# Hybrid mLSTM/attention/MoE trunk: the router reads the residual row without its norm, between the blocks of the output projection, and the slot lists are built by one-hot matmuls

## What is computed

```python
x = post_norm(x, concat([ya, yb, yc]) @ w_out[l], g_a, ln_g[l, 0], ln_b[l, 0])   # LayerNorm(ALPHA*x + gate*y)
h = x * (1.0 + sc_f) + sh_f
x = post_norm(x, moe_ffn(h, w_router_grp[l], w_router_exp[l], ...), g_f, ln_g[l, 1], ln_b[l, 1])

def moe_ffn(h, w_rg, w_re, w_g, w_u, w_d):
    pg = softmax(h @ w_rg); grp = argmax(pg); g_w = max(pg)          # 1 of 4 groups
    le = (h @ w_re).reshape(T, 4, 8)[own group]
    top_l, top_i = top_k(le, 2); top_w = softmax(top_l) * g_w        # 2 of its 8 experts
    ...                       # each expert: (silu(xb @ w_g[e]) * (xb @ w_u[e])) @ w_d[e], on its own tokens
    y = segment_sum(out[pos] * w_s)
```

## Time and profile before

| | |
|---|---|
| median of 3 runs | 1881.56 us (1878.47 to 1889.72) |
| the profiled execution | 1880.61 us |
| its span | 1878.7 us, 22715 instructions |
| PE matmul busy | 1457.2 us (78%) |
| PE weight load busy | 1014.3 us (54%) |
| DVE / ACT / POOL busy | 605.1 / 338.9 / 411.3 us |
| chain that ended last, by engine | PE 61%, DMA 19%, DVE 10%, issue 4%, POOL 3% |

### The profile page before, as it was taken

How to read it: one execution, slowest core, us unless ns; L and a number is a source line. 1 busy time by engine, 2 the same in 40 slices (tenths; PEclk the granted TensorE clock), 3 DMA queues, 4 the chain that set the end, 5 groups by cost and what they waited for, 6 DMA issues and landing times.

```text
span 1878.7 us, 22715 instructions
## 1 busy us (share of the span) xinstructions
PE 1457.2 (78%) x8398; PEld 1014.3 (54%) x8398; DVE 605.1 (32%) x1375; ACT 338.9 (18%) x854; POOL 411.3 (22%) x552
## 2 busy tenths in 40 slices
PE   5999999687973798897049999978798548998730
PEld 2888888465862333332048888855587514333210
DVE  0301232764353112111542123247725412111144
ACT  0211112463010111111012111225511001111001
POOL 1000041522172111111130000525215231112113
PEclk9999999799965899998579999989898569999865
DMA  9112436125053699996412133431123529999832
GB/s 354 49 72 76 165 118 238 48 76 192 11 221 149 234 407 412 396 394 274 165 45 76 54 121 136 171 121 43 35 90 140 229 102 377 418 399 410 343 122 100
DMA packets 76252, 356.19 MB, mean 190 GB/s; under 512 B 21776, under 2 KB 25008, under 8 KB 41200
## 3 DMA queue, kind: packets, MB, share of 16 engines
q1 hardware_dynamic: 41040, 291.63, 39.3%
q0 software_dynamic: 22528, 48.74, 7.6%
q10 hardware_dynamic: 12576, 14.37, 2.4%
HBM read 344.28 MB, written 33.16 MB: 201 GB/s over the span
## 4 chain that ended last, share of the span: by engine, by line
PE 61%; DMA 19%; DVE 10%; issue 4%; POOL 3%; ACT 1%; SPq 1%; DVEq 0%; POOLq 0%; ACTq 0%
PE bank L894 22%; PE bank L1188 10%; PE bank L1105 7%; DMA att<-h_rows,cur 7%; DMA ring<-in_w_exp 4%; PE bank L1207 3%; PE bank L697 2%; PE bank L1172 2%; DMA z<-expert_rows 2%; DMA ring<-in_w_ada 2%; PE bank L1052 1%; DMA att<-bias_full 1%; PE bank L712 1%; PE bank L1126 1%; DMA z<-in_w_exp 1%
## 5 line engine op out<-in xcount | busy, mean ns | idle before, releaser
L894 PE MATMUL bank<-ring,hT 128*128 128x256 f32 (+1 forms) x1920 | 411.3, 373 | 3.6 <-DVE hT L1585 3.6
L894 PEld LDWEIGHTS bank<-ring,hT 128*128 128x128 f32 x1920 | 350.5, 190 | 48.2 <-issue 5.2
L1188 PE MATMUL bank<-ring,att 128*64 128x512 f32 (+1 forms) x512 | 166.0, 635 | 19.8 <-DMA ring<-in_w_exp 19.8
L1105 PE MATMUL bank<-ring,hT 128*128 128x256 f32 x640 | 138.6, 379 | 2.4 <-issue 2.4
L1105 PEld LDWEIGHTS bank<-ring,hT 128*128 128x128 f32 x640 | 121.4, 190 | 19.0 <-issue 2.6
L1188 PE MATMUL bank<-z,att 128*64 128x512 f32 x512 | 121.4, 629 | 11.5 <-DMA z<-in_w_exp 11.4
L1188 PEld LDWEIGHTS bank<-ring,att 128*64 128x64 f32 (+1 forms) x512 | 61.6, 168 | 109.8 <-issue 109.8
L2077 DVE TENSOR_TENSOR att<-att,bank 128x256 f32<-128x256 f32 x38 | 16.0, 421 | 304.9 <-ACT att L1512 304.9
L1757 DVE COPY z<-bank 128x512 f32<-128x512 f32 (+3 forms) x36 | 21.0, 583 | 260.0 <-PE bank L894 260.0
L2345 POOL COPY cur<-att 128x1 int32<-128x1 int32 (+1 forms) x38 | 6.9, 181 | 392.9 <-ACT att L1519 293.8
L1172 PE MATMUL bank<-const,att 128*128 128x128 f32 x320 | 52.7, 319 | 43.4 <-DMA att<-h_rows,cur 41.6
(11 more groups left out here) (319 smaller groups left out, 2112.9 us busy)
## 6 DMA issues: line engine op xcount, KB each, us to landing
ring<-in_w_exp SPq DMA_DIRECT2D x96, 1024.0 KB, 15.8
z<-in_w_exp SPq DMA_DIRECT2D x96, 1024.0 KB, 13.6
ring<-in_w_ada SPq DMA_DIRECT2D x48, 1024.0 KB, 5.0
ring<-in_w_in SPq DMA_DIRECT2D x24, 1024.0 KB, 7.0
z<-expert_rows ACTq DMA_DIRECT2D x20, 512.0 KB, 4.3
ring<-in_w_out SPq DMA_DIRECT2D x8, 1024.0 KB, 10.2
z<-mod_rows POOLq DMA_DIRECT2D x12, 512.0 KB, 8.6
h_rows<-z POOLq DMA_DIRECT2D x10, 512.0 KB, 2.9
```

Of the source, the lines that this page charges most:

```text
L894: last = eng.matmul(bk[:, i * UN:i * UN + nw], hTv[:, k, t * P:(t + 1) * P], w[:, k, 0:nw], start=(k == 0), stop=(k == KD - 1))
L1105: last = eng.matmul(bk[:, i * UN:(i + 1) * UN], hTv[:, k, t * P:(t + 1) * P], w[2 * half + i][:, k, :], start=(k == 0), stop=(k == KD - 1))
L1188: last = eng.matmul(bank[2 + j][c * m_:(c + 1) * m_, :], e["xT"][:, j, k * P + c * m_:k * P + (c + 1) * m_], wv[c][:, 0:2, k, :], start=(k ...
```

## The change

**The router reads x without its norm.** With u = ALPHA*x + gate*y, the row h is linear in u for a given mean and rstd, so h @ w = rstd * (u @ W') - mean*rstd * colsum(W') + b'w, with W' = w times ln_g*(1+sc_f) and b' = ln_b*(1+sc_f) + sh_f. `router_weights` makes the two scaled copies of the router weights for the two kinds of rows (`lr["wx"]`) on DVE in the attention loop behind unit 4. `router_sums` takes their column sums on PE (8 matmuls of 144 columns) at i = 16. ln_g and ln_b in column form come from a transpose at the start of the program. RT now transposes x itself as soon as u is there, and RL multiplies by wx.

**Order.** PE does RT and RL of tile t-1 between the blocks of the projection of tile t. The choice of experts is made in two parts: tiles 0 to 3 (`choose(0)`) on DVE between the two residuals of tile 4, tile 4 (`choose(1)`) behind its logits. The rank matmuls are in two parts too, the first 10 between RT and RL of tile 4, with wider moving operands (6 of 64 to 128 columns, 4 of one), and 3 after the second choice.

**Rows for the experts.** POOL folds ln_g and ln_b into the scale and shift rows once (6 products and sums of 1024, event `rows`); then h comes from the centred row in two operations. `ln_gain` and `ln_shift` of tiles 3 and 4 are moved behind the slots and behind the first two gathers, the loads of the next norm rows too. The final routing weights (`weights_of_two`) are made last.

**Slot lists.** Slot numbers are compared with multiples of 128 (which pass) and with 0..127 (which place); 10 matmuls of a 128x128 one-hot by a 128x31 one-hot times (token number + 1) sum up to the transposed lists in PSUM. The DRAM lists, their first fill and their 10 scatters are gone.

**Loads.** SP issues expert weights 2 when u of tile 4 and `rows` are there, and weights 3 when the last RL is full. Two masks now come to z by two loads at the start, and ACT's first copy waits for them in place of the fill of the DRAM lists.

```diff
-                eng.wait_ge(*ev.at("full", jobs.number(("RL", l, NT - 1))))
-                eng.wait_ge(*ev.at("st_h2", l, NT - 2))
-                eng.wait_ge(*ev.at("st_h2", l, NT - 1))
+                eng.wait_ge(*ev.at("u", l, NT - 1))
+                eng.wait_ge(*ev.at("rows", l))
...
+                    if n == 3:
+                        eng.wait_ge(*ev.at("full", jobs.number(("RL", l, NT - 1))))
...
+                def rows_turned(t):
...
+                        eng.wait_ge(*ev.at("u", l, t))
                         for k in range(4):
-                            last = eng.transpose(bk[:, k * P:(k + 1) * P],
-                                                 m["hs"][:, t % 2, (4 * j + k) * P:(4 * j + k + 1) * P], ident)
+                            last = eng.transpose(bk[:, k * P:(k + 1) * P], x[:, t, (4 * j + k) * P:(4 * j + k + 1) * P], ident)
...
+                for t in range(NT):
+                    for half in range(2):
+                        jobs.open("Y", l, t, half)
+                        eng.wait_ge(*jobs.room())
+                        project(t, half, 0)
+                        if half == 0 and t > 0:
+                            rows_turned(t - 1)
+                        project(t, half, 1)
+                        if half == 0 and t > 0:
+                            logits(t - 1)
+                rows_turned(NT - 1)
+                ranks(0)
+                logits(NT - 1)
+                ranks(1)
...
+                for k in range(2):
+                    eng.wait_ge(*ev.at("hot", l, k))
+                    for t in range(NT):
+                        n = k * NT + t
+                        last = eng.matmul(bk[:, 0:NLIST], hot["slot"][:, n, :], hot["pass"][:, n, :], start=(n == 0),
+                                          stop=(n == 2 * NT - 1))
...
+            def router_weights(l):
...
+                for part, col in enumerate((gcol, bcol)):
+                    for g in range(2):
+                        last = eng.tensor_tensor(lr["wx"][:, :, 2 * part + g, :], wr[:, :, :], bc(col[:, g, :], 2, 36), ALU.mult)
...
                 for t in range(NT):
+                    if t > 0:
+                        turned_half(t - 1)
+                        logit_fix(t - 1)
+                    residual(t, 0)
+                    if t > 0:
+                        logit_rows(t - 1)
+                    if 0 < t < NT - 1:
+                        expert_rows(t - 1)
+                        ln_gain(1, t - 1)
+                    if t == NT - 1:
+                        choose(0)
+                    residual(t, 1)
+                    ln_stats(1, t)
+                turned_half(NT - 1)
+                logit_fix(NT - 1)
+                expert_rows(NT - 2)
+                logit_rows(NT - 1)
+                choose(1)
+                expert_rows(NT - 1)
...
-                eng.tensor_copy(posi[:, :], s5[:, 8:10, :].rearrange("p a b -> p (a b)")).then_inc(*dve.event("slots", l))
+                eng.tensor_tensor(hot["ge"], bc(at, 2, 32), bc(K["iopass"], 1, 2 * NT), ALU.is_ge).then_inc(*dve.step())
...
+                    eng.tensor_tensor(hot["slot"][:, ns, :], bc(within[:, ns], 2, P), bc(K["iop"], 1, NT),
+                                      ALU.is_equal).then_inc(*dve.event("hot", l, k))
...
+                for g in range(2):
+                    eng.tensor_tensor(m["free"][:, g, :], lr["scsh"][:, 0, g, :], m["ln"][:, 1, :], ALU.mult).then_inc(*pool.step())
+                    eng.wait_ge(*pool.last())
+                    eng.tensor_tensor(lr["scsh"][:, 1, g, :], lr["scsh"][:, 1, g, :], m["free"][:, g, :], ALU.add)
+                    last = eng.tensor_tensor(lr["scsh"][:, 0, g, :], lr["scsh"][:, 0, g, :], m["ln"][:, 0, :], ALU.mult)
+                last.then_inc(*pool.event("rows", l))
...
                 for t in range(NT):
+                    if 0 <= t - 1 < NT - 2:
+                        store_rows(t - 1)
+                    ln_rstd(1, t)
+                    if 0 <= t - 1 < NT - 2:
+                        ln_shift(1, t - 1)
+                store_rows(NT - 2)
...
-                for q in range(2 * NT):
-                    eng.indirect_dma_start(list_dram[l], bass.IndirectOffsetOnAxis(ap=posi[:, q:q + 1], axis=0),
-                                           ids[:, q:q + 1], None).then_inc(*pool.event("list_in", l, q, by=16, sem="list_in"))
-                eng.wait_ge(*ev.at("list_in", l, 2 * NT - 1))
-                ld(listi, list_dram[l].rearrange("(b p) o -> b (p o)", p=P), "list_back", l)
```

458 lines of the change are left out of this document (262 added, 196 removed).

## The result

| | before | changed |
|---|---|---|
| median | 1883.22 us (4 runs, 1878.47 to 1889.72) | 1823.88 us (4 runs, 1821.26 to 1824.33) |
| ratio | | 0.9682, 95% interval 0.9658 to 0.9706 |
| span of the profiled execution | 1878.7 us | 1819.4 us |

The account below looks back on a forecast made before the run. PE, busy 78% of the span, was taken as the bound. Projection to first pass: 119.2 us against 157.4; less 3.5 for attention, 34.7 gained per layer, 69.1 in all with the start: 1812 us, range 1796 to 1835.

Parts of the forecast that it names:

- Projection, 83 us at clock 1.00: Sign of being right: the projection with four RT and four RL inside takes 83 us at full clock.
- The first tile, 1.5 us: Early in the projection, PE stalls ahead of RT(1) for u(1), behind POOL's first rstd: about 1.5 us, 0 to 6.
- waits of 1 to 2 us are harmless to the clock: In the projection, planned PE waits of 1 to 2 us lie below what the trace shows to be harmless.
- Clock halved throughout (the other side): Rival: transposes between projection matmuls halve PE's clock; throughout, 69.3 us more per layer, 1951 us; chance 0.05.
- No interleaving: Rival: in the projection RL takes 3.6 us, POOL's six operations 3.21 each; +11 us per layer, 1834 us; chance 0.12.
- The split: choose(0), at most 5.7 us on DVE, hides behind 6.9 us of projection; its failure (1823 us) is within the 0.66.
- Ranks at E + 12.1: Behind the projection's end (E), the ranks are ready after 12.1 us, where before it was 55.6.
- Slots at E + 20.5: After the ranks, the same 8.4 us of short PE/DVE exchanges put the slots 20.5 us behind the projection's end (E).
- Lists, 8.5 us: From slots to slot lists, DVE comparisons and ten one-hot matmuls at half clock take 8.5 us, before 18.4.
- First gather: From lists to first pass, 5.7 us before plus 1.5 for busy DMA; first pass 36.2 us behind the projection's end.
- the DMA rival: Rival: weight loads, stores of h and gather collide ahead of the first pass; +9 us per layer, 1830 us; chance 0.13.
- Gain outside: In the attention, router_weights (+1.5) and router_sums (+2.0) cost 3.5 us per layer, bounds 1.5 and 6.

Follow-up runs that it names:

- e3: Changed kernel with POOL adding the shift of the expert rows of tiles 3 and 4 on only 64 of 1024 columns: 1820.5 us.
- e4: Changed kernel with the load of the fourth weight buffer waiting for the first gather's landing in place of the last logits: 1824.2 us.

## Why the prediction was right, and where it was off

- **The sign and the mechanism.** Right. Both parts undone one at a time give it back: the place of the router 19 us per layer with the split choice (5.4 at the ranks) in it, the lists 15. They add up to 34, beside the 33.6 and 33.2 gained between the start of the projection and the first pass; but each was undone with the other in place, so this sum could as well have missed. That the router reads the row without its norm was not undone alone; it is what allows the place.
- **Projection, 83 us at clock 1.00.** RT 0.87 to 1.04 and RL 1.71 to 1.87 us stood against 1.04 and 2.0 in the sum; 79.9 us without any stall, 81.5 predicted. The measured 83.9 and 85.0 come from the term of the first tile.
- **The first tile, 1.5 us.** The wait was 2.07 and 2.98 us, within its bounds of 0 to 6, but the term's own pieces don't give its 1.5: rstd at 28 and 5.8 us of DVE work make u(1) 33.8, ahead of PE's 34.2. In layer 0 rstd came at 28.5 and u(1) at 35.9; most of what the pieces lacked is the hold of 1.4 us on the second residual, by POOL's addition for tile 0. And the sentence that waits of 1 to 2 us are harmless to the clock failed. It rested on the earlier trace rows, where the clock fell 4.5 us (I read 5) after dense work ended; that showed when it falls in a long pause, not that a short one is safe. Each fall cost 1.7 us, and each wait 0.2 beyond its length. Term 1.5, measured 3.9 and 4.9.
- **Clock halved throughout (the other side).** Refuted: 1.00 over the whole projection where no wait stands in it, with the four RT between the blocks. **No interleaving** too: RL was never 3.6 us in the projection.
- **The split.** `choose(0)` took 5.5 us (5.7 at most, predicted) and was over 1.0 us before Y(4,1) was full.
- **Ranks at E + 12.1.** Measured 13.2; the 1.1 is the hold at L2017. **Slots at E + 20.5.** Measured 23.2: the 8.4 us of short exchanges became 10.0, the 1.6 is the hold at L2093. I had taken both times over from rows in which POOL stood idle, and didn't ask what POOL does there now. This is the step that failed: a stage that "stays the same" had got a neighbour. The first tile failed by the same step, 1.4 us more.
- **Lists, 8.5 us.** Measured 8.45, with 4.4 for ten matmuls at half clock as in the sum.
- **First gather.** 7.2 us from lists to first pass, measured 8.15 and 7.7: the DMA rival in small. Its mechanism is real, and stronger than the sum had it: with the holds removed (e3) the gather absorbs all of the 2.8 us, and with the gather freed (e4) POOL's `ln_shift` absorbs 1.9 and 1.6 us of the 2.2 and 1.5 gained.
- **Gain outside.** 3.5 us per layer for the attention: 0.2 and 2.6 in the two profiles, 3.6 and 3.3 against the means of ten, so of the right size and no better known than that. The expert stage as long as before: 347.9 us against 347.6 to the transposes of layer 1, 352.1 against 351.1 in layer 1.

Together: first tile 2.4 and 3.4 us, holds 2.7 twice, gather 1.0 and 0.5, less 1.6 twice on the cheaper RT and RL: 4.5 and 5.0 us per layer, the 10 us that the forecast lacked against the profiled execution.
